# Gate and up products of five gated layers as seven half-size products in place of eight, activation halves made in the down stage

## The reference

```python
D_FF = 2816
h2 = rmsnorm(x, norm_ffn_g[l])
x = x + (jax.nn.silu(h2 @ w_gate[l]) * (h2 @ w_up[l])) @ w_down[l]
```

## Time and profile before

| | us |
|---|---|
| median of 3 runs | 3099.9 (3097.95 to 3100.64) |
| the profiled execution | 3100.87 |
| its span | 3099.2 |
| TensorE busy | 3079.5 |
| VectorE busy | 1559.8 |
| ScalarE busy | 948.3 |

### The profile page before, as it was taken

How to read it: one execution, slowest core, us unless ns; L and a number is a source line. 1 busy time by engine, 2 the same in 40 slices (tenths; PEclk the granted TensorE clock), 3 DMA queues, 4 the chain that set the end, 5 groups by cost and what they waited for, 6 DMA issues and landing times.

```text
span 3099.2 us, 35866 instructions
## 1 busy us (share of the span) xinstructions
PE 3079.5 (99%) x14821; PEld 2546.8 (82%) x14821; DVE 1559.8 (50%) x1681; ACT 948.3 (31%) x1060; POOL 50.5 (2%) x148
## 2 busy tenths in 40 slices
PE   9999999999999999999999999999999999999998
PEld 8878888888888888888888888788888878888887
DVE  7975443465554443466544424655443455454433
ACT  3473221343332222344322222223221343332213
POOL 5100000000000000000000000000000000000000
PEclk9999999999999999999999999999999999999999
DMA  5122332342132223212322233223332221233222
GB/s 182 47 75 82 96 116 94 102 136 69 53 97 95 95 95 102 89 55 63 101 95 95 95 102 98 86 81 98 98 103 89 93 78 62 73 101 99 98 88 75
DMA packets 250513, 282.79 MB, mean 91 GB/s; under 512 B 11874, under 2 KB 216864, under 8 KB 250408
## 3 DMA queue, kind: packets, MB, share of 16 engines
q1 hardware_dynamic: 250408, 281.30, 28.2%
HBM read 279.16 MB, written 4.73 MB: 92 GB/s over the span
## 4 chain that ended last, share of the span: by engine, by line
PE 91%; DVE 5%; ACT 1%; issue 1%; POOL 1%; DMA 0%; SPq 0%; ACTq 0%; DVEq 0%
PE ps L1857 26%; PE ps L1859 26%; PE ps L1858 26%; PE ps L2421 1%; PE ps L2423 1%; PE ps L2422 1%; PE ps L2339 1%; PE ps L2357 1%; DVE wlo L1145 1%; ACT whi L684 1%; PE ps L2347 1%; PE ps L2402 1%; PE ps L2381 1%; PE ps L2282 1%; PE ps L2302 1%
## 5 line engine op out<-in xcount | busy, mean ns | idle before, releaser
L1857 PE MATMUL ps<-hh,whi 128*128 128x512 f32 x2496 | 981.6, 393 | 0.0
L1859 PE MATMUL ps<-hh,wlo 128*128 128x512 f32 x2496 | 972.1, 389 | 0.0
L1858 PE MATMUL ps<-hl,whi 128*128 128x512 f32 x2496 | 971.8, 389 | 0.0
L1145 DVE TENSOR_TENSOR wlo<-raw,whi 128x2048 fp32r<-128x2048 f32 (+2 forms) x274 | 591.0, 2157 | 631.9 <-ACT whi L684 631.5
L684 ACT ACTIVATE whi<-raw 128x2048 fp32r<-128x2048 f32 (+2 forms) x274 | 494.7, 1806 | 1159.9 <-PE ps L1859 1130.6
L1857 PEld LDWEIGHTS ps<-hh,whi 128*128 128x128 f32 x2496 | 468.6, 188 | 101.8 <-issue 4.4
L1859 PEld LDWEIGHTS ps<-hh,wlo 128*128 128x128 f32 x2496 | 468.5, 188 | 98.7
L1858 PEld LDWEIGHTS ps<-hl,whi 128*128 128x128 f32 x2496 | 468.8, 188 | 96.5 <-issue 0.7
L1857 PE MATMUL ps<-act,whi 128*128 128x512 f32 x1264 | 494.6, 391 | 1.3 <-DVE wlo L1145 0.9
L1859 PE MATMUL ps<-act,wlo 128*128 128x512 f32 x1264 | 491.9, 389 | 0.0
L1858 PE MATMUL ps<-act,whi 128*128 128x512 f32 x1264 | 491.9, 389 | 0.0
(11 more groups left out here) (385 smaller groups left out, 2323.9 us busy)
## 6 DMA issues: line engine op xcount, KB each, us to landing
raw<-in_w_ffn_in SPq DMA_DIRECT2D x88, 1024.0 KB, 5.1
raw<-in_w_in SPq DMA_DIRECT2D x59, 1024.0 KB, 5.3
raw<-in_w_ffn_out SPq DMA_DIRECT2D x40, 1024.0 KB, 5.0
raw<-in_w_o SPq DMA_DIRECT2D x32, 640.0 KB, 4.0
raw<-in_w_gate SPq DMA_DIRECT2D x11, 1024.0 KB, 5.2
raw<-in_w_up SPq DMA_DIRECT2D x11, 1024.0 KB, 5.3
raw<-in_w_down SPq DMA_DIRECT2D x10, 1024.0 KB, 5.0
raw<-in_w_mem_kv SPq DMA_DIRECT2D x8, 1024.0 KB, 5.2
```

The source lines that it names most:

```text
L1145: v.tensor_tensor(wlo[:, u % 2, 0:n], raw[:, u % 2, 0:n], whi[:, u % 2, 0:n].bitcast(F32), ALU.subtract).then_inc(lo_made, 1)
L1857: mm(dst, wh, xh, start=first, stop=False, skip_group_check=True)
L1858: mm(dst, wh, xl, start=False, stop=False, skip_group_check=True)
L1859: return mm(dst, wl, xh, start=False, stop=last, skip_group_check=True)
```

## The change

Pairs 0 and 1 of each network stay as they were (but without the split of their product). From pair 2 on, 18 units a network, a unit's 1024x256 matrix is seen as four blocks: A11 (even k tiles, first 128 output features), A12 (odd k tiles, first 128), A21 (even, last 128), A22 (odd, last 128). h is seen as four blocks too (even or odd k tiles, first or last 256 tokens). Instead of eight block products there are seven, in the scheme with S1 = A21 + A22, S2 = S1 - A11, S3 = A11 - A21, S4 = A12 - S2, and four sums of h made once a network (`traw`, split in `th` and `tl`). One product is 4 k tiles x 3 matmuls of 256 columns (`product`), so a unit is 84 matmuls of 256 columns.

VectorE makes the four sums of a unit (into `stmp`), ScalarE the high halves of the seven **forms** (`wh8`, 8 places of 512 columns where `whi` was), VectorE their low halves (`wl8`). Each form has one place, so a form of the next unit is written when its product of this unit is done. Partial results that enter two outputs are copied out of PSUM by ScalarE (`snap_taken`, three of 256 columns a unit), and VectorE finishes a unit's output in four operations. `raw` keeps its two slots, and SyncE's program is the same, instruction by instruction.

The products in TensorE's order for unit m are A11, S3 of unit m-1, S1, A12, S2, A22 of unit m-1, S4. The gated product is kept in fp32 (`actr`, without `rstd` on the up side from pair 2 on). In the down stage VectorE first scales it (`down_lows`, 4 tiles a unit, units 0 to 5), ScalarE makes the high half of the 4 tiles (`act_high`), VectorE the low half (`act_low`), in two ring buffers.

```diff
+
+        HALF = T // 2
+        banks_of = ps[:, :].rearrange("p (b n) -> p b n", b=8)
+        ABANK, BBANK, DBANK = (2, 5), (4, 6), (3, 7)
+        FORM = {"A11": 0, "S1": 1, "A12": 2, "S2": 3, "S4": 4, "S3": 5, "A22": 6}
+        STREAMED = 9
+
+        def place_of(form, p):
+
+            return (FORM[form] + 4 * p) % 8
...
+        def corner(slot, form):
+
+            two, n0 = {"A11": (0, 0), "A12": (1, 0), "A21": (0, P), "A22": (1, P)}[form]
+            return raw[:, slot, :].rearrange("p (k two n) -> p k two n", two=2, n=256)[:, :, two, n0:n0 + P]
```

VectorE's order for one unit, m = 2i + j:

```diff
+            def seven(s, u0, gc, i, j):
+
+                p, first = u0 % 2, isinstance(i, int) and i == 0 and j == 0
+                last = isinstance(i, int) and i == STREAMED - 1 and j == 1
+                slot, g = (u0 + 4 + j) % 2, 1 - j
+                pair = None if first or not g else tiles_of_pair(i)
+                form = 91 * s + 5 * j + 4
+                sum_s3(p, slot)
+                if not last:
+                    dve.wait_ge(loaded[1 - slot], at_turn(i, 16, 16 * ((u0 + 5 + j) // 2 + 1)))
+                    sum_s1(p, 1 - slot)
+                if not first:
+                    take_c12(s, i, g, (109 * s + 6 * j, 54 * s + 3 * j))
+                if not last:
+                    corner_low("A11", p, 1 - slot, form_hi, at_turn(i, 10, form + 1), form_lo)
+                if not first:
+                    take_c22(s, i, g, (109 * s + 6 * j + 2, 54 * s + 3 * j - 1))
+                if not last:
+                    dve.wait_ge(sum_made, at_turn(i, 8, 76 * s + 4 * j + 9))
+                    sum_s2(p, 1 - slot)
+                if not first:
+                    dve.wait_ge(late_made, at_turn(i, 4, 36 * s + 2 * j))
+                    finish_late(s, i, g, pair)
+                if last:
+                    sum_low("S3", p, 91 * s + 90)
+                else:
+                    sums_low("S1", "S3", p, at_turn(i, 10, form + 2))
+                    corner_low("A12", p, 1 - slot, form_hi, at_turn(i, 10, form + 3), form_lo)
+                    dve.wait_ge(sum_made, at_turn(i, 8, 76 * s + 4 * j + 10))
+                    sum_s4(p, 1 - slot)
+                if not first:
+                    dve.wait_ge(unit_used, at_turn(i, 2, u0 + 4 + j))
+                    finish_early(s, i, g, pair)
+                corner_low("A22", p, slot, form_hi, 91 * s + 91 if last else at_turn(i, 10, form + 4), lo_made)
+                if not last:
+                    sums_low("S2", "S4", p, at_turn(i, 10, form + 5))
...
+            def down_lows(s, u0, ds):
+
+                for d in ds:
+                    if d < 6:
+                        n, t = 2 if d == 5 else 4, 4 * d
+                        v.tensor_tensor(actr[:, t:t + n, :], actr[:, t:t + n, :], bc(rstd[:, :], n), ALU.mult).then_inc(act_scaled, 1)
+                    low(u0 + 22 + d)
+                    act_low(s, d)
```

ScalarE's order for one unit (`corner_high`, `sum_high` and `sums_high` make the high halves of one form, one, or two):

```diff
+            def act_high(s, u0, d):
+
+                act.wait_ge(unit_used, u0 + 22 + d - 1)
+                if d < 6:
+                    act.wait_ge(act_scaled, 5 * s + d)
+                n = 2 if d % 6 == 5 else 4
+                t = 4 * (d % 6)
+                a.activation(ringh[d % 2][:, 0:n, :], actr[:, t:t + n, :], ACT.Copy).then_inc(ffn_hi, 1)
...
+                done = lambda k: act.wait_ge(product_done, at_turn(i, 12, 109 * s + 6 * j + k))
+                slot = (u0 + 4 + j) % 2
+                done(1)
+                a.activation(bank(BBANK[j], HALF), bank(ABANK[j], HALF), ACT.Copy).then_inc(snap_taken, 1)
+                if not last:
+                    raw_here(u0, i, 5 + j)
+                    corner_high("A11", p, 1 - slot, form_hi)
+                if j == 0 and not first:
+                    act.wait_ge(acc_free, at_turn(i, 2, gc + 3))
+                    a.activation(gs[:, :, :], gs[:, :, :], ACT.Silu).then_inc(silu_done, 1)
+                done(3)
+                if first:
+                    act.wait_ge(act_step, 2 * s + 2)
+                else:
+                    act.wait_ge(late_made, at_turn(i, 4, 36 * s + 2 * j))
+                a.activation(us[:, 1, 0:HALF], bank(DBANK[j], HALF), ACT.Copy).then_inc(snap_taken, 1)
+                act.wait_ge(sum_made, at_turn(i, 8, 76 * s + 4 * j + (8 if last else 9)))
+                if last:
+                    sum_high("S3", p)
+                else:
+                    sums_high("S1", "S3", p)
+                    done(4)
+                    corner_high("A12", p, 1 - slot, form_hi)
+                done(5)
+                if not first:
+                    act.wait_ge(late_made, at_turn(i, 4, 36 * s + 2 * j - 1))
+                a.activation(us[:, 0, 0:HALF], bank(BBANK[j], HALF), ACT.Copy).then_inc(snap_taken, 1)
+                act.wait_ge(unit_used, at_turn(i, 2, u0 + 4 + j))
+                corner_high("A22", p, slot, form_hi)
+                if not last:
+                    act.wait_ge(sum_made, at_turn(i, 8, 76 * s + 4 * j + 11))
+                    done(6)
+                    sums_high("S2", "S4", p)
```

TensorE:

```diff
+                form = lambda k: pe.wait_ge(form_lo, at_turn(i, 8, 73 * s + 4 * j + k))
+                if not tail:
+                    form(1)
+                    pe.wait_ge(acc_free, at_turn(i, 2, gc + 3 + j))
+                    product("A11", p, h11, ABANK[j], start=True).then_inc(product_done, 1)
+                if not first:
+                    form(1 if tail else 2)
+                    pe.wait_ge(snap_taken, at_turn(i, 6, 54 * s + 3 * j))
+                    product("S3", p, t_(3), BBANK[1 - j]).then_inc(product_done, 1)
+                if not tail:
+                    form(2)
+                    if first:
+                        pe.wait_ge(ffn_lo, 19 * s + 4)
+                    product("S1", p, t_(1), DBANK[j], start=True, open_sem=product_done if first else None).then_inc(product_done, 1)
+                    form(3)
+                    pe.wait_ge(snap_taken, at_turn(i, 6, 54 * s + 3 * j + 1))
+                    product("A12", p, h21, ABANK[j]).then_inc(product_done, 1)
+                    form(4)
+                    product("S2", p, t_(2), BBANK[j]).then_inc(product_done, 1)
+                if not first:
+                    pe.wait_ge(lo_made, at_turn(i, 2, u0 + 4 + j))
+                    pe.wait_ge(late_made, at_turn(i, 4, 36 * s + 2 * j))
+                    product("A22", p, t_(4), BBANK[1 - j]).then_inc(unit_used, 1)
+                if not tail:
+                    pe.wait_ge(snap_taken, at_turn(i, 6, 54 * s + 3 * j + 2))
+                    product("S4", p, h22, DBANK[j]).then_inc(product_done, 1)
+
             def swiglu(s, u0, gc, r):
                 first_turn(r, u0, 4, 0)
-                with pe.Fori(1, FF // 256) as i:
+                for j in range(2):
+                    unit_ready(u0 + 2 + j)
```

More of the change, by code:

```diff
@@ new lines, in swiglu @@
+                dve.wait_ge(ffn_hi, 26 * s + KD)
+                tiles = hg[:, :, :].rearrange("p (k two) n -> p k two n", two=2)
+                b11, b12, b21, b22 = (tiles[:, :, k, HALF * h:HALF * h + HALF] for k in range(2) for h in range(2))
+                t1, t2, t3, t4 = (traw[:, k, :, :] for k in range(4))
+                v.tensor_tensor(t1, b12, b11, ALU.subtract).then_inc(sum_made, 1)
+                v.tensor_tensor(t3, b22, b12, ALU.subtract).then_inc(sum_made, 1)
+                dve.wait_ge(sum_made, 76 * s + 1)
@@ new lines, in swiglu, with turn @@
+                sum_s4(p, p)
+                corner_low("A12", p, p, form_hi, 91 * s + 3, form_lo)
+                up_out(1)
+                sums_low("S2", "S4", p, 91 * s + 4)
+                gated(1)
+                def turn(i):
+                    for j in range(2):
+                        seven(s, u0, gc, i, j)
+                turn(0)
+                with dve.Fori(1, STREAMED - 1) as i:
+                    turn(i)
+                turn(STREAMED - 1)
+                take_c12(s, STREAMED, 1, (109 * s, 54 * s))
@@ L2214, in memory_turned, with product @@
                     e.then_inc(S("mem_tr"), 1)
+            def product(form, p, moving, b, start=False, open_sem=None):
+                q = place_of(form, p)
+                for k in range(KD // 2):
+                    w = slice(P * k, P * k + P)
+                    xh_, xl_ = moving(k)
+                    for m, (wgt, xx) in enumerate(((wh8, xh_), (wh8, xl_), (wl8, xh_))):
+                        e = mm(bank(b, HALF), wgt[:, q, w], xx, start=start and k == 0 and m == 0,
+                               stop=k == KD // 2 - 1 and m == 2, skip_group_check=True)
+                        if open_sem is not None and k == 0 and m == 0:
+                            e.then_inc(open_sem, 1)
+                return e
@@ L2245, in swiglu @@
                 pe.wait_ge(rstd_ready, 3 * (r + 1))
[L2246 removed]
+                loop(pe, 2, down, peel=2)
             swiglu(0, U_GU1, G_GU1, 1)
```

350 lines of the change are left out of this document (267 added, 83 removed).

## The result

The changed kernel takes 3224.68 us (median of 4 runs, 3224.42 to 3225.43), the kernel before 3100.18 us (median of 4 runs, 3097.95 to 3100.64). The ratio is 1.0402, with a 95% interval of 1.039 to 1.0415: **124.5 us slower**. 3237 us were predicted, with 3195 to 3285 as the range.

A forecast was written before the change was run, and what follows sets the result against it. The prediction took TensorE to bound the kernel before, and the load in line with VectorE's work to bound the changed units. 5 x (26.0 + 1.4) = 137 us on 3100.87, less 1.0 for the median, gave 3237 us, range 3195 to 3285.

The forecast's parts named there:

- What TensorE saves: Gate and up units: 84 matmuls at 0.120 us, 10.08 us a unit instead of 10.88, 72 us over 90 units.
- The load is what does not fit: Gate and up units: the load waits for A22's low half and S1 waits for the load, 12.43 us a unit.
- The size of the line: From A22's low half of one unit to the next: 5.30 + 6.75 + 0.38 = 12.43 us, 1.55 more than before.
- The load's part: From A22's low half's end to S1's start: issue 0.16, landing 5.1, start 0.04, sum 5.30 us.
- The unknown prices: VectorE's corner reads (at most +61 us) and register instructions before waits (up to +24 us), both taken as nothing.
- Start and end of a network: Eighteen gate and up units: down stage starts at 221.8 us instead of 195.84, +26.0 us a network.
- The down stage: Full units keep 10.88 us; unit 6 comes late, 1.4 us a network; possible lateness of unit 7 left out.
- Faster: Rival, gate and up units: the load comes before VectorE wants it, unit 10.08 us, kernel 3040 us; chance 0.04.
- Nothing overlaps: Rival, VectorE's chain: each of eleven operations costs its whole length, 13.28 us a unit, 3305 us; chance 0.03.
- Dearer waits: Rival, VectorE's chain: registers and some corners cost more, 12.7 to 13.0 us a unit, 3260 to 3285 us; chance 0.17.
- Cheaper chain: Rival, gate and up units: load of 4.8 us or no 0.38 wait, or both, 3180 to 3218 us; chance 0.12.
- The clock: Rival, gate and up units: TensorE's granted clock falls to 1.2 GHz and TensorE bounds, 3830 us; chance 0.02.

The follow-up runs named there:

- a22_early: Changed kernel with a second place for form A22, used in turn by even and odd units, its low half made right behind S3; 3053.77 us, ratio 0.9851.

## Why the prediction was right

By its own steps:

- **What TensorE saves.** 0.120 us a matmul, so 10.08 a unit: right. The kernel after hides it; `a22_early` shows it (184.83 us for 18 units, 10.13 from A11 to A11 at the mean).
- **The load is what does not fit.** Right in kind, in place and in direction, by three runs: the load shortened by 1.58 us shortens the unit by 1.59; 0.6 us more in the line costs 48 us and beside it 5; with the line cut the load costs nothing.
- **The size of the line.** 12.43 us predicted. Measured from A11 of unit 2 to A11 of unit 17, at the mean: 12.44 in the first network, 12.25, 12.29, 12.31 and 12.25 in the others. That the first network meets 12.43 is in part luck, since its loads take 5.3 us and not 5.1. In the unit shown above, of 12.21: operations ahead of A22's low half and the low half itself: 6.75 predicted, 6.79 measured (6.99 less the wait). The wait for S1/S3's high half: 0.38 predicted, 0.20 measured. The load's part: 5.30 predicted, 5.22 measured. The largest miss is the wait. From C22's end (2266.96) to S1/S3 low (2268.36) are 1.40 us where four pieces were added up to 1.51; ScalarE's copy of 256 elements out of PSUM took 0.39 and not 0.47. VectorE's own two operations there end 1.20 us after the same point, where 1.13 was taken.
- **The unknown prices.** A corner read costs nothing over a plain one (0.68 to 0.69, next operation 0.60 later). Register instructions ahead of waits cost nothing that shows. Both were taken as nothing, right.
- **Start and end of a network.** A22's low half of unit 0 ends 9.05 us behind the first A11 in the second network (9.4 predicted), which is mostly a slip: the 3.9 us taken for VectorE's end of pair 1 are more than the terms named for it (0.20 + 1.14 + 1.14 + 1.23 = 3.71), and 3.61 were measured. A11 of unit 2 starts at 20.8 (21.3), A11 of unit 17 at 204.5 (207.8), the down stage at 218.4 (221.8), so the end takes 13.9 us (14.0). Over the five networks the stretch is 219.3 at the mean, 2.5 us less than predicted, which makes 12.6 us in all, about the whole difference between 137 and 124.5. The first network alone is at 221.44; its loads, from `w_gate` and `w_up`, land in 5.3 us and not in 5.0.
- **The down stage.** 1.4 us a network predicted, 1.2 measured, and 1.5 ahead of unit 7 in the first network, which the prediction had named as possible and left out. 7.0 against 7.5.
- **Where TensorE stands idle.** 1.7 ahead of A11 and 0.7 ahead of A22 predicted; 1.3 and 0.3 by the records, 1.5 and 0.5 against the pace.
- **The rivals.** Faster: falls, the load was the one thing in its way. Nothing overlaps (3305): falls, the spacing is 0.60. Dearer waits: falls, they were a little cheaper. Cheaper chain: it was to bring 11.7 to 12.2 a unit; the 12.25 to 12.31 of four networks lie just above that, so the measured time, 3224.7, stands between this rival (up to 3218) and the 3237 of the sum. The clock: didn't fall for good, see below.

By the Trainium skill, "DMA: Bandwidth & Descriptors", section "Anatomy of one DMA", whose fit is for loads issued by GpSimd, a load of 1024 KB takes an estimated 4.4 us and the kernel an estimated 3181 us. The trace, of loads issued by SyncE, disagrees: 5.0 at the median, and 3.5 for 512 KB.

By the Trainium skill, "VectorE: DVE Perf Modes", section on the TRN2 errata, an operation's fixed part is exposed between instructions; worked out for the chain, so that each operation costs its whole length, that is an estimated 3305 us. The length agrees with the trace (0.69), the exposure doesn't: the additional operation in the line cost 0.60.

## What to carry to other kernels

When an engine's early operation in a unit reads what a transfer brings, and the transfer waits for a late operation of the same engine, the two are one ring: its time is their sum, whatever the engines' busy shares are. Look for the last reader of each buffer, not only for its first, and move that reader ahead; here one empty place of 2 KB a partition in each of two buffers turned +4.0% into -1.5%. With one ring cut, look for the next: it can close over two units, and then half of what an engine saves comes back. A step added to such a ring costs its full spacing every turn, the same step beside it next to nothing (48 us and 5 us here), so two runs with one dummy operation in either place tell a ring from a full engine.
